# The new tokens of each decoded sequence as eight more key columns, and the first sequence's softmax moved up into the prompt heads

## The reference, cut to what matters

```python
def one_seq(args):
    qn, qr, cn, krn, pages = args
    c_all = jnp.concatenate([cache_c[pages].reshape(n_past, KV_LORA), cn], axis=0)      # 1024 + 8 rows
    kr_all = jnp.concatenate([cache_kr[pages].reshape(n_past, QK_ROPE), krn], axis=0)
    q_lat = jnp.einsum('thd,rhd->thr', qn, w_uk)
    s = (jnp.einsum('thr,lr->htl', q_lat, c_all)
         + jnp.einsum('thr,lr->htl', qr, kr_all)).astype(jnp.float32) * ATTN_SCALE
    s = jnp.where(mask[None], s, -jnp.inf)
    p = jax.nn.softmax(s, axis=-1)
    o_lat = jnp.einsum('htl,lr->thr', p, c_all)
    return jnp.einsum('thr,rhd->thd', o_lat, w_uv)
```

## Time and profile before

| what | value |
|---|---|
| median of three runs | 1988.13 us |
| the profiled execution: time, span | 1988.56 us, 1986.6 us |
| PE busy | 1959.0 us (99%) |
| DVE, ACT busy | 1092.2 us (55%), 761.2 us (38%) |
| mean granted TensorE clock | 0.996 of full speed |
| chain that ended last | 97% PE |
| prompt heads, PE's first score to its last value product | 606.0 to 671.6 us |
| from turn(0) to the end of sequence 6's values | 680.8 to 793.5 us |

### The profile page before, as it was taken

The page is one execution under the profiler, slowest core; times in us unless marked ns, Lnnn a source line. Parts: engine busy times, 40 slices in busy tenths (PEclk is TensorE's granted clock), DMA queues, the critical chain, the costliest instruction groups (busy, mean ns, idle before and its releaser), DMA issues.

```text
span 1986.6 us, 33915 instructions
## 1 busy us (share of the span) xinstructions
PE 1959.0 (99%) x13368; PEld 1935.2 (97%) x13368; DVE 1092.2 (55%) x1469; ACT 761.2 (38%) x836; POOL 48.8 (2%) x188
## 2 busy tenths in 40 slices
PE   8999999999999899999999999999999999999997
PEld 8999999999998799999999999999999999999997
DVE  6865344333335764355556655555556555565656
ACT  5356542332246654233334232333323333333334
POOL 1002000000000000000000000000000000000000
PEclk9999999999999999999999999999999999999998
DMA  6444444444444487454444434344444444444443
GB/s 248 142 151 178 148 148 148 148 149 148 149 173 157 141 281 285 149 202 149 149 150 158 163 136 161 148 148 148 148 148 148 148 149 148 146 153 143 159 140 121
DMA packets 59878, 318.13 MB, mean 160 GB/s; under 512 B 6514, under 2 KB 6834, under 8 KB 27186
## 3 DMA queue, kind: packets, MB, share of 16 engines
q1 hardware_dynamic: 58882, 312.85, 44.5%
q10 hardware_dynamic: 944, 4.57, 0.6%
HBM read 313.08 MB, written 4.32 MB: 160 GB/s over the span
## 4 chain that ended last, share of the span: by engine, by line
PE 97%; DVE 1%; ACT 1%; DMA 1%; issue 0%; SPq 0%; DVEq 0%; ACTq 0%
PE ps L1434 96%; PE ps L1729 0%; DVE w_lo L884 0%; DMA xT<-in_x 0%; DVE y_gain L884 0%; DMA w_raw<-in_cache_t 0%; DVE neg_max L1191 0%; ACT w_hi L484 0%; DVE sm L1185 0%; ACT sm L706 0%; SPq L359 0%; DVE k_rope L884 0%; ACT qlat L484 0%; PE ps L1672 0%; ACT pt L484 0%
## 5 line engine op out<-in xcount | busy, mean ns | idle before, releaser
L884 DVE TENSOR_TENSOR w_lo<-w_raw,w_hi 128x2048 fp32r<-128x2048 f32 (+2 forms) x270 | 608.1, 2253 | 453.8 <-ACT w_hi L484 453.5
L1434 PE MATMUL ps<-h_hi,w_hi 128*128 128x320 f32 x2512 | 742.0, 308 | 9.1 <-ACT w_hi L484 9.1
L484 ACT ACTIVATE w_hi<-w_raw 128x2048 fp32r<-128x2048 f32 (+2 forms) x272 | 508.4, 1870 | 624.5 <-PE ps L1434 624.2
L1434 PE MATMUL ps<-h_lo,w_hi 128*128 128x320 f32 x2512 | 741.2, 309 | 0.0
L1434 PEld LDWEIGHTS ps<-h_hi,w_hi 128*128 128x128 f32 x2512 | 473.0, 188 | 9.6 <-ACT w_hi L484 9.1
L1434 PEld LDWEIGHTS ps<-h_lo,w_hi 128*128 128x128 f32 x2512 | 471.5, 188 | 0.5 <-DVE h_lo L985 0.3
L1434 PE MATMUL ps<-h_hi,w_lo 128*128 128x320 f32 x2496 | 391.1, 308 | 0.0
L1434 PEld LDWEIGHTS ps<-h_hi,w_lo 128*128 128x128 f32 x2496 | 372.5, 187 | 0.0
L1434 PE MATMUL ps<-hid_hi,w_hi 128*128 128x320 f32 x704 | 216.5, 308 | 0.0
L1434 PE MATMUL ps<-hid_lo,w_hi 128*128 128x320 f32 x704 | 216.5, 308 | 0.0
L1434 PE MATMUL ps<-hid_hi,w_lo 128*128 128x320 f32 x704 | 216.5, 307 | 0.0
(11 more groups left out here) (230 smaller groups left out, 1766.7 us busy)
## 6 DMA issues: line engine op xcount, KB each, us to landing
w_raw<-in_slabs SPq DMA_DIRECT2D x253, 1024.0 KB, 4.8
w_raw<-in_cache_t SPq DMA_DIRECT2D x64, 288.0 KB, 4.1
c_raw<-in_cache SPq DMA_DIRECT2D x56, 256.0 KB, 4.8
w_whole<-in_slabs SPq DMA_DIRECT2D x4, 1024.0 KB, 7.0
x_again<-in_x ACTq DMA_DIRECT2D x1, 2560.0 KB, 9.8
c_last<-in_cache SPq DMA_DIRECT2D x8, 256.0 KB, 4.2
xT<-in_x SPq DMA_DIRECT2D x3, 640.0 KB, 8.6
out_y<-y_gain SPq DMA_DIRECT2D x2, 640.0 KB, 3.1
```

What stands on the lines that cost most here:

```text
L484: return nc.scalar.activation(out, in_, ACT.Copy)
L884: return nc.vector.tensor_tensor(out, a, b, op)
L1434: return nc.tensor.matmul(out, a, b, start=start, stop=stop, **kw)
```

## The change

A sequence's key buffers become one tile `keys_hi` and one `keys_lo` of 128 x 4 x 1032 (by latent part, then by token), which lie where `w_hi[0]`, `w_hi[1]` and `w_lo[0]`, `w_lo[1]` lie; the eight last columns are the sequence's own new tokens, written by a small copy on ACT (`new_key_hi`) and a small subtraction on DVE (`new_key_lo`). The rotary keys become `k_rope_all`, 128 x 1032. The scores of sequences 1 to 7 are made in three chunks: 512 columns, 256 columns, and 264 columns (256 cached and the own 8) into bank 7. `new_scores` is left for sequence 0 alone, with 8 columns in place of 64, in step 15 of the prompt heads. The mask now spreads the own eight scores over 64 columns.

```diff
+KEYS = PAST + NT
+CHUNKS = ((0, 4 * PAGE), (4 * PAGE, 6 * PAGE), (6 * PAGE, KEYS))
...
+            def new_key_hi(b):
+                if b > 1:
+                    act.wait_ge(slab_used, GS + 2 * b)
+                copy(keys_hi[:, :, PAST:], new_columns(b))
+                copy(k_rope_all[:, PAST:], kr_new[:, b * NT:(b + 1) * NT]).then_inc(key_new_hi, 1)
...
             # ACT, prompt heads
+                if i == 16:
+                    new_key_hi(1)
                 if i == 17:
+                    exp_scores(0)
                     act.wait_ge(slab_used, GS + 2)
                     key_rope_hi(1, 1)
...
-            exp_scores(0)
-            act.wait_ge(slab_used, GS + 2)
             query_hi(2)
```

DVE in the prompt heads: the low halves of sequence 0's first keys move from steps 7 and 8 to 9 and 11 (they now cover the whole slabs of the latent queries, so they wait for all of these), and mask, maximum and normalising of sequence 0 come in:

```diff
+                    if i == 16:
+                        dve.wait_ge(mask_step, 2)
+                        mask_new(0)
                     tt(o_lo[:, h, 0:NP], ps[:, 6 + h % 2, 0:NP], o_hi[:, h, 0:NP], ALU.subtract).then_inc(olo_done, 1)
...
                 if i == 7:
-                    dve.wait_ge(slab_used, G0["ukt"] + UKT_ORDER.index(2) + 1)
                     key_rope_lo(0, 0)
-                if i in (7, 8):
-                    key_lo(0, 0, i - 7)
+                if i == 9:
+                    dve.wait_ge(slab_used, GS)
+                    key_lo(0, 0, 0)
                 if i == 10:
                     query_lo(0)
+                if i == 11:
+                    key_lo(0, 0, 1)
...
+                if i == 16:
+                    dve.wait_ge(slab_used, GS + 2)
+                    maximum(0)
                 if i == 17:
                     key_rope_lo(1, 0)
-                if i in (18, 19):
-                    key_lo(1, 0, i - 18)
+                    key_lo(1, 0, 0)
+                if i == 18:
+                    normalise(0)
+                    key_lo(1, 0, 1)
+
+            query_lo(2)
+            new_key_lo(1)
```

PE:

```diff
+                    if i == 15:
+                        pe.wait_ge(krn_lo, 1)
+                        new_scores()
...
-                if i == 17:
-                    pe.wait_ge(sc_masked, H)
+                if i == 16:
+                    pe.wait_ge(sc_masked, H - 1)
                     score_high(1, 0)
...
+            def last_scores(b):
+                pe.wait_ge(spt_act, b)
+                pe.wait_ge(key_new_lo, b)
+                score_high(b, 2)
+                score_low(b, 2).then_inc(slab_used, 1)
...
-            new_scores(0)
+            pe.wait_ge(olo_done, H)
             for i in range(1, NB):
                 b = i - 1
                 if i == 1:
-                    score_low(i, 0)
+                    score_low(i, 0).then_inc(slab_used, 1)
                     score_high(i, 1)
+                    score_low(i, 1)
                     turn(b)
-                    score_low(i, 1)
                 else:
                     pe.wait_ge(sx_done, 2 * (i - 1))
-                    score(i, 0)
+                    score_high(i, 0)
+                    score_low(i, 0).then_inc(slab_used, 1)
                     turn(b)
-                    score(i, 1)
-                new_scores(i)
+                    score_high(i, 1)
+                    score_low(i, 1)
+                last_scores(i)
```

```diff
+            sp.dma_start(vec[:, :], vecs).then_inc(gain_in, 16)
+            x_tiles(0, 0, 1, x_first)
             sp.dma_start(*latent_rows(0, 0, 1)).then_inc(slab0_part[0], 16)
...
-            act.dma_start(vec[:, :], vecs).then_inc(gain_in, 16)
-            act.dma_start(xT[:, 0:1, :], x[:, 0:1, :]).then_inc(x_first, 16)
```

More of the change, by code:

```diff
@@ L136, in program @@
         scale_in = sb("scale_in", [P, T])
-        k_rope = [sb(f"k_rope{s}", [P, QUAD, PAGE], F32R, at=norm_reg + 2048 * s) for s in range(2)]
+        k_rope_all = sb("k_rope_all", [P, KEYS], F32R, at=norm_reg)
+        k_rope = [k_rope_all[:, s * QUAD * PAGE:(s + 1) * QUAD * PAGE].rearrange("p (a t) -> p a t", a=QUAD)
+                  for s in range(2)]
         nmx = sb("neg_max", [P, 2 * H])
@@ L337, in _ @@
             stream(RT, G0["ukt"])
+            sp.wait_ge(kr_ready, 1)
+            sp.dma_start(page_sb[:, :], pages).then_inc(pages_in, 16)
             held = {}
@@ L765, in _ @@
                 copy(spt[:, 0:PAST // 2], ps[:, 4, :])
-                copy(spt[:, PAST:], ps[:, 7, P:2 * P]).then_inc(spt_act, 1)
+                copy(spt[:, PAST:], ps[:, 7, 3 * P:]).then_inc(spt_act, 1)
                 if i + 1 < NB:
@@ L898, in key_lo @@
                 at = slice(2 * half, 2 * half + 2)
-                out, src = page_halves(w_lo, q)
-                last = tt(out[:, at], src[:, at], page_halves(w_hi, q)[0][:, at], ALU.subtract)
+                out, src = page_halves(keys_lo, q)
+                last = tt(out[:, at], src[:, at], page_halves(keys_hi, q)[0][:, at], ALU.subtract)
                 if half:
@@ L1175, in _, with new_key_lo, mask_new @@
             nc.vector.tensor_copy(new_mask[:, NS - NT:NS], const("mask_new", NT)).then_inc(mask_step, 1)
+            def new_key_lo(b):
+                dve.wait_ge(key_new_hi, b)
+                tt(keys_lo[:, :, PAST:], new_columns(b), keys_hi[:, :, PAST:], ALU.subtract).then_inc(key_new_lo, 1)
+            def mask_new(i):
+                if i:
+                    dve.wait_ge(slab_used, GS + 2 * i + 2)
+                else:
+                    dve.wait_ge(ss_done, 1)
+                first = NS - NT - NT * i
+                tt(new_score[:, :].rearrange("p (b t) -> p b t", b=NB), own_scores(i),
+                   new_mask[:, first:first + NS].rearrange("p (b t) -> p b t", b=NB), ALU.add).then_inc(sn_done, 1)
@@ L1623, in score_out @@
             def score_out(b, q):
-                out = ps[:, 2 * (b % 2) + q, :]
-                return out, out.rearrange("p (a c) -> p a c", a=QUAD)
-            def key_tiles(w, q):
-                t = w[q][:, :].rearrange("p (a j c) -> p j a c", a=QUAD, j=RT)
-                return [t[:, r] for r in range(RT)]
+                k0, k1 = CHUNKS[q] if b or q == 0 else (CHUNKS[1][0], PAST)
+                return (ps[:, 7, 0:k1 - k0] if q == 2 else ps[:, 2 * (b % 2) + q, 0:k1 - k0]), slice(k0, k1)
@@ L1650, in score_low, with new_scores @@
-                mm(out, rope_query(q_rope_lo, b), keys, False, True).then_inc(slab_used, 1)
+                    mm(out, ql_hi[:, b % 2, r * P:(r + 1) * P], keys_lo[:, r, at], False, False)
+                mm(out, rope_query(q_rope_hi, b), k_rope_all[:, at], False, False)
+                return mm(out, rope_query(q_rope_lo, b), k_rope_all[:, at], False, True)
+            def new_scores():
+                out = ps[:, 6, NP:NP + NT]
+                for r in range(RT):
+                    mm(out, qlat[:, 0, r, :], c32[:, r, NP:NP + NT], r == 0, False)
+                mm(out, rope_query(q_rope_hi, 0), kr_new[:, 0:NT], False, False)
+                mm(out, rope_query(q_rope_lo, 0), kr_new[:, 0:NT], False, True).then_inc(ss_done, 1)
@@ L1694, in _ @@
                 if i == 12:
[L1695 removed]
+                    score_low(0, 0).then_inc(slab_used, 1)
                 if i == 14:
@@ L1706, in _ @@
             pe.wait_ge(krn_lo, 1)
-            def score(b, q):
-                score_high(b, q)
-                score_low(b, q)
-            def new_scores(i):
-                out = ps[:, 7, 0:NS]
-                if i:
-                    pe.wait_ge(spt_act, i)
-                else:
-                    pe.wait_ge(olo_done, H)
-                for r in range(RT):
-                    mm(out, qlat[:, i, r, :], c32[:, r, NP:T], r == 0, False)
-                mm(out, rope_query(q_rope_hi, i), kr_new[:, :], False, False)
-                mm(out, rope_query(q_rope_lo, i), kr_new[:, :], False, True).then_inc(ss_done, 1)
+            def last_scores(b):
[3 more added lines that the diff above has]
+                score_low(b, 2).then_inc(slab_used, 1)
             def turn(b):
```

149 lines of the change are left out of this document (87 added, 62 removed).

## The result

| | before | after |
|---|---|---|
| median of five runs each, same chip | 1988.08 us | 1977.89 us |
| range | 1987.0 to 1988.9 | 1977.34 to 1978.43 |
| profiled execution: time, span | 1988.56, 1986.6 us | 1978.37, 1976.5 us |

The ratio is 0.9948, 95% interval 0.9937 to 0.996: 10.2 us less, where 6.9 were forecast. The direction was right; the 3.3 us between are the subject of what follows.

The account below looks back on a forecast made before the run. PE, busy 99% of the span, was taken to bound the kernel. Terms -5.7 + 0.2 - 0.6 - 1.0 + 0.2 = -6.9 us took 1988.13 to 1981.2 us; 8-in-10 range 1977.8 to 1985.5.

Parts of the forecast that it names:

- Part 1: Sequence loop: three score chunks replace two plus new_scores, -0.95 us a turn; -5.7 us for turns 2 to 7.
- Part 2: Shorter loop turn: DVE, ACT and fetches must keep up; values' second-half fetch tightest; +0.2 us, range 0 to 3.
- sign of being wrong: Forecast wrong if turns last over 16 us, or passage and start together give more than 4 us or lose.
- (b): Sequence loop: fetch or DVE's chain sets turns of 16.2 us or more, half of part 1 lost; 1984.2 us, chance 0.18.
- Part 3: Passage from prompt heads to sequence loop: reordered softmax and splits, turn 1's saving included; -0.6 us, range -3 to +1.5.
- Part 4: Kernel start: vec and first x tile first on SP's queue, PE's flow 1.0 us sooner; -1.0 us, range -2 to +0.9.
- Part 5: Last turn, turn(7): nothing hides its normalising chain, which gets longer; +0.2 us.
- (a): Passage gains all: PE's gaps close and clock stays up, -4 to -5.7 us there; 1977.5 us, chance 0.13.
- (c): Key copies, written in 16 runs of 128 floats a slab, get dearer; slower, 1993.5 us, chance 0.05.

Follow-up runs that it names:

- e3: Changed kernel with w_hi 128 bytes higher, so w_hi and w_lo stand 16384 bytes apart as before; 1981.72 us.
- a0: The changed kernel again, unedited, timed beside the kernel before on the same chip; 1978.26 us, ratio 0.9951 to before.
- e1: Kernel before with only the changed kernel's memory places (w_lo, vec, constants) and late page numbers; 1983.45 us, ratio 0.9975 to before.
- e6: Changed kernel, but the values wait for each page of c_raw by itself, not all four of a half; 1975.64 us.
- e5: Changed kernel with sequence 0's softmax put back behind the last prompt head, as before; 1978.26 us.
- e9: Kernel before with the changed kernel's memory places and its start (e1 plus vec and first x tile first on SP's queue); 1984.04 us.
- e8: Changed kernel with another order of PE's and DVE's work between prompt heads and sequence loop; 1976.96 us.
- e12: Changed kernel with e6's page waits, e8's passage order, w_lo's products between w_hi's in most one-output slabs, and w_hi 128 bytes higher; 1980.67 us.

## Why the prediction was right and where it was wrong

**What was missing (the failed step).** The sum has no term for the new places of `w_lo`, `vec` and the constants. The prediction priced the key tiles as columns and copies; of the stages outside the two attentions it looked at the start alone, and put the rest at nothing without a reason. Measured: 3.5 us (e3 against a0) to 5.4 us (e1 against before), of which the traces show 3.6 in the spacing of untouched products. A second term was wrong the other way: the start, forecast at -1.0 us, gave 0. The two together, 2.5 to 4.4 us, are the miss of 3.3 us.

**Part 1, the columns: right, -1.0 us a turn.** The undisturbed turn is 15.63 us, 1.03 less. A cut in three chunks costs nothing, the 264-column products start 0.12 us apart. I had taken 0.95 to be cautious; in e6, without stalls, six turns give 94.01 - 87.91 = 6.1 us (5.7 forecast).

**Part 2, the fetch: the right place, the wrong size.** I found the four DMAs of the values' second half to be what is tightest, and took 0.2 us. Measured against e6 it is 1.8 us, inside the range of 0 to 3 that stood there. The slack of 1.2 us was reckoned from a landing time of 4.8 us, the median of all. The wait is for the last of four, and the trace of before had the number: the four of the earlier trace rows took 5.1 to 6.7 us, so there was hardly any slack. In the changed kernel such transfers took up to 6.3. Its turns took 15.93, 15.95, 16.40, 15.63 and 16.05, two of them above the 16 us that the prediction names as a sign of being wrong: this is rival (b) in small, by the fetch and not by DVE, whose slack stayed at 1.7 us. The loop gave 4.35 us, against 5.7 - 0.2 - 0.2 = 5.3.

**Part 3, the passage: about right.** -0.6 forecast, -1.0 in the two profiles, -1.2 in the mean of more (above), where turn 1's `new_scores` alone should give 1.0. With a scatter of 1.7 us between profiles the close hit is partly luck. The waits came as named, 3.94 us for o_lo (3.9 forecast), 0.85 for spt (0.9), the one for the split only 0.3 in place of 3.0: DVE was done with it at 676.5, not 678.8, and the half level, 6.8 us of it in place of 3.4, slowed the products ahead. That the move of the softmax gives nothing of its own (e5) was the point of the working.

**Part 4, the start: the first product right, the term wrong.** The first product came at 7.25 (7.1 forecast) and the profiles of before and after differ by 1.0 us; timed by itself the start is worth 0 within 0.4. The step that failed is the one from the early tile to "PE's flow comes 1.0 us sooner". One profile of a start was not enough to price it.

**Part 5, the last turn: its +0.2 us did not come.** turn(6) to turn(7) fell from 10.72 to 9.74 us, the full gain of a turn.

**Rivals.** (a) is refuted by e5 in its mechanism, though its 1977.5 us is nearest to the result: a right number for a wrong reason. (c) is refuted by 1916 and 2291 ns. (b) holds for half of its 3 us: 1.6 us more than forecast, by the fetch. In sum, by the runs: columns and passage -5.8 (e9 against after), start 0, places -3.5 to -5.4, together -9.3 to -11.2; measured -10.2. That columns and passage came out at -5.8, where the terms add up to -5.9, is partly luck: the columns, the last turn and the passage gave 0.4, 0.2 and about 0.5 us more than forecast, and the fetch took 1.6 more.

## What to carry to other kernels

When a change grows or moves a tile, list which tiles get another address or another distance from each other, and put a term for it into the forecast with both signs; compare the spacing of untouched products first when the traces of before and after are laid side by side. A wait for a group of transfers is a wait for the last of them, so let the consumer wait by the piece that it uses (in e6 the same fetch then cost nothing), and reckon its slack from the last landing, not from the median. A gain ahead of a stage that is fed by transfers can be lost there: e8 kept 1.3 of 3.1 us. Take a trace of before twice when a term is read from its start or from a passage with waits.

## What the runs showed of the hardware

With the low weights 16384 bytes behind the high ones, three kinds of products of 320 columns in the down projection start 146.5 to 146.8 ns apart, in all five kernels of that kind; with 16512 bytes they start 147.9, 143.7 and 145.1 ns apart. 16448 and 16480 are no better than 16384. It repeats to 0.01 us a chunk. With 16512 the order of the products in the other slabs is worth 0.4 us in 84.24, with 16384 0.00 in 84.48. Products of 256 columns start 117.8 ns apart in four kernels with 16384 and 113.6 with 16512, but about 113.4 in e12 with 16384: something else has a part there. The difference is about the same where DVE and ACT stand idle. The mechanism is open. The half level of PE's clock in the same passage lasted from nothing (e9) to 6.8 us (the changed kernel), and moved what followed by up to 1.7 us.
